# One mixture-of-experts block: first weights fetched a stage earlier, first products moved ahead of the second rows

## The reference

```python
x_mid = x + g1 * y                                   # y = merged @ w_o
h2 = modulate(rmsnorm(x_mid, norm_ffn), sh2, sc2)
g_logits = hf @ w_rg + b_rg                          # 4 groups
e_logits = hf @ w_re + b_re                          # 32 experts
...                                                  # top group, top 2 experts in it
row_tok = zeros(P).at[dest].set(tok_s)               # rows sorted by expert, blocks of 128
def run_block(tok, e, wt):
    xb = h[tok]
    y = (silu(xb @ w_g[e]) * (xb @ w_u[e])) @ w_d[e]
    return y * wt[:, None]
```

## Time and profile before

| | us |
|---|---|
| three runs, median (lowest, highest) | 1725.38 (1722.64, 1728.64) |
| the profiled execution, whole | 1726.99 |
| its span on the core | 1724.9 |
| PE busy | 1585.3 (92%) |
| DVE busy | 1181.1 (68%) |
| ACT busy | 835.0 (48%) |
| POOL busy | 185.5 (11%) |

### The profile page before, as it was taken

The page is one execution under the profiler, slowest core; times in us unless marked ns, Lnnn a source line. Parts: engine busy times, 40 slices in busy tenths (PEclk is TensorE's granted clock), DMA queues, the critical chain, the costliest instruction groups (busy, mean ns, idle before and its releaser), DMA issues. The chain is left out here.

```text
span 1724.9 us, 21049 instructions
## 1 busy us (share of the span) xinstructions
PE 1585.3 (92%) x7666; PEld 1303.0 (76%) x7666; DVE 1181.1 (68%) x1406; ACT 835.0 (48%) x912; POOL 185.5 (11%) x173
## 2 busy tenths in 40 slices
PE   7999899979939999999999999397999799999995
PEld 5789677767838888888888888276866588888883
DVE  7787866636368989898888988276666833434346
ACT  2412243362237788888888787242333523222222
POOL 0000000000021232323323231000000000000000
PEclk8999999989969999999999999698999899999998
DMA  8242344423178999999999997533102132323201
GB/s 320 89 155 87 103 147 156 166 74 101 46 285 284 367 369 366 372 378 371 378 367 368 366 369 281 198 110 120 50 27 71 52 100 93 99 96 97 98 25 49
DMA packets 121576, 329.88 MB, mean 191 GB/s; under 512 B 12601, under 2 KB 80313, under 8 KB 96817
## 3 DMA queue, kind: packets, MB, share of 16 engines
q1 hardware_dynamic: 110450, 312.11, 50.0%
q0 software_dynamic: 11072, 17.03, 2.9%
HBM read 333.00 MB, written 20.99 MB: 205 GB/s over the span
## 5 line engine op out<-in xcount | busy, mean ns | idle before, releaser
L1453 DVE TENSOR_TENSOR moe_expert_lo<-moe_expert_raw,moe_expert_hi 128x2048 fp32r<-128x2048 f32 x124 | 281.2, 2289 | 57.5 <-ACT moe_expert_hi L1275 57.5
L1275 ACT ACTIVATE moe_expert_hi<-moe_expert_raw 128x2048 fp32r<-128x2048 f32 x124 | 234.8, 1920 | 25.4 <-PE moe_bank L1548 24.0
L1535 PE MATMUL moe_bank<-moe_expert_lo,moe_x_hi 128*128 128x512 f32 x512 | 202.6, 396 | 0.0
L1536 PE MATMUL moe_bank<-moe_expert_hi,moe_x_lo 128*128 128x512 f32 x512 | 199.7, 390 | 0.0
L1537 PE MATMUL moe_bank<-moe_expert_hi,moe_x_hi 128*128 128x512 f32 x512 | 199.7, 390 | 0.0
L1865 ACT ACTIVATE second_c_hi<-second_c_raw 128x2048 fp32r<-128x2048 f32 x44 | 84.0, 1909 | 162.5 <-PE second_bank L2320 161.2
L2318 PE MATMUL second_bank<-second_cx_lo,second_c_hi 128*128 128x512 f32 x352 | 141.0, 400 | 15.4 <-DVE second_cx_lo L2015 10.2
L827 PE MATMUL mixer_bank<-mixer_h_lo,mixer_w_hi 128*128 128x512 f32 x320 | 132.2, 413 | 10.7 <-DVE mixer_h_lo L577 10.7
L2319 PE MATMUL second_bank<-second_cx_hi,second_c_lo 128*128 128x512 f32 x352 | 138.5, 393 | 0.0
L2320 PE MATMUL second_bank<-second_cx_hi,second_c_hi 128*128 128x512 f32 x352 | 138.3, 393 | 0.0
L2318 PE MATMUL second_bank<-g_lo,second_c_hi 128*128 128x512 f32 x320 | 127.4, 398 | 1.2 <-DVE g_lo L2153 1.2
(11 more groups left out here) (405 smaller groups left out, 3186.2 us busy)
## 6 DMA issues: line engine op xcount, KB each, us to landing
moe_expert_raw<-in_w_exp_up_dram SPq DMA_DIRECT2D x64, 1024.0 KB, 7.6
moe_expert_raw<-in_w_exp_down_dram SPq DMA_DIRECT2D x62, 1024.0 KB, 7.3
second_c_raw<-in_w_mlp_dram SPq DMA_DIRECT2D x32, 1024.0 KB, 5.3
moe_shared<-in_w_exp_gate_dram SPq DMA_DIRECT2D x31, 1024.0 KB, 7.1
work<-in_w_exp_gate_dram SPq DMA_DIRECT2D x31, 1024.0 KB, 7.1
mixer_raw<-in_w_in_dram SPq DMA_DIRECT2D x18, 1024.0 KB, 5.1
mixer_raw<-in_w_mod_t_dram SPq DMA_DIRECT2D x16, 1024.0 KB, 4.9
second_c_raw<-in_w_in_dram SPq DMA_DIRECT2D x8, 1024.0 KB, 8.7
```

The costliest lines, as they stand in the source:

```text
L1275: act_e.activation(w_hi[q][:], raw[r], ACT.Copy).then_inc(hi_done, 1)
L1453: dve.tensor_tensor(w_lo[q][:], raw[r], w_hi[q][:].bitcast(F32), ALU.subtract)\
L1535: pe.matmul(out, x_hi[s][:, c, :], lo[:, k, :], start=(h == 0 and k == 0), stop=False)
L1536: pe.matmul(out, x_lo[s][:, c, :], hi[:, k, :], start=False, stop=False)
```

## The change

It has four parts. `vals` and `kq` are now allocated around both stages, and four of the six raw buffers are parts of them; SP fetches the first expert's four units at the end of `mixer_stage`, behind the last `w_o` unit and a wait for the merged branches' last split (`mlo_done`). In `moe_stage` SP issues the stores first and the next expert's two gate units behind them. PE does both halves of block 0's gate ahead of `transpose_x(1, 0)`, and ACT and DVE take their splits in a matching order. In the mixer, `router(5)` and `router(6)` go into the last tile, behind chunks 3 and 6. Besides, some small tables lie in free parts of `vals` and `kq`, and DVE waits first for one of POOL's tables (`back4`), later for the rest.

```diff
@@ mixer_stage, SP
+            sp.wait_ge(mlo_done, KC)
+            for n, src in enumerate((w["w_exp_gate"], w["w_exp_gate"], w["w_exp_up"], w["w_exp_up"])):
+                sp.dma_start((vals if n < 2 else kq)[:, 2048 * (n % 2):2048 * (n % 2) + 2048],
+                             src[0].rearrange("e (p h k) f -> e h p (k f)", p=P, h=2)[0:1, n % 2])\
+                  .then_inc(expert_landed[n], 16)
@@ mixer_stage, PE
                             ins = feature_chunk(dst[:], s, k, h_hi, h_lo, c)
+                            if s == NS - 1 and k == 1 and c in (3, 6):
+                                router(KC - 3 if c == 3 else KC - 2)
...
-                    if s > 22:
+                    if s > 22 and (s, k) != (NS - 1, 1):
                         router(2 * (s - 22) + k - 2)
...
-            router(KC - 2)
@@ moe_stage
-        raw = [sb(f"expert_raw{i}", [P, 2048]) for i in range(RAW - 2)]
+        raw = [t[:, 2048 * i:2048 * i + 2048] for t in (vals, kq) for i in range(2)]
@@ moe_stage, SP
-            for n, src in enumerate((wg, wg, wu, wu)):
-                expert_unit(None, n, src, 0, n % 2)
-            expert_unit(None, 5, wg, 1, 1)
-            sp.wait_ge(xst_evac, KC)
-            expert_unit(None, 4, wg, 1, 0)
             for t in range(TC):
                 sp.wait_ge(h2_ready, t + 1)
                 sp.dma_start(dram["h2"][t * 128:(t + 1) * 128, :], h2_rows[:, t, :]).then_inc(h2_stored, 16)
+            for n in range(2):
+                expert_unit(None, 4 + n, wg, 1, n)
@@ moe_stage, POOL
-            numbers(back4[:], [[-1, 4]], 4, 0)
+            numbers(back4[:], [[-1, 4]], 4, 0).then_inc(back_ready, 1)
@@ moe_stage, ACT
             first_hi(2)
-            first_hi(3)
             act_e.wait_ge(gd_ready, 1)
             act_e.activation(gexp[:], gexp[:], ACT.Exp)
             act_e.activation(e2[:], e2[:], ACT.Exp).then_inc(gexp_ready, 1)
             x_high(0, 0)
+            first_hi(3)
+            split_hi(0, 0, 0)
             x_high(1, 1)
-            split_hi(0, 0, 0)
@@ moe_stage, DVE
-            dve.wait_ge(tables_ready, 1)
+            dve.wait_ge(back_ready, 1)
...
+            dve.wait_ge(tables_ready, 1)
             dve.tensor_tensor(chosen[:], iota_row[:, 0:32].unsqueeze(2).to_broadcast([P, 32, 8]),
...
             first_lo(1)
+            x_low(0, 0)
             first_lo(2)
-            token_gates()
-            x_low(0, 0)
-            x_low(1, 1)
             first_lo(3)
             split_lo(0, 0, 0)
+            x_low(1, 1)
+            token_gates()
             split_lo(0, 0, 1)
@@ moe_stage, PE
             pe.wait_ge(xlo_done, 1)
-            transpose_x(1, 0)
             for h in range(2):
                 pe.wait_ge(lo_done, RAW + h + 1)
                 gate_like(bank[2][:], 0, h, h).then_inc(unit_used, 1)
+            transpose_x(1, 0)
```

43 lines of the change are left out of this document (23 added, 20 removed).

## The result

| | before | after |
|---|---|---|
| runs | 12 | 12 |
| median (lowest, highest), us | 1726.59 (1722.64, 1730.61) | 1731.91 (1727.95, 1735.40) |
| ratio to before, 95% interval | | 1.0031 (1.0019 to 1.0043) |
| the profiled execution, whole / span, us | 1726.99 / 1724.9 | 1733.67 / 1731.6 |

The changed kernel is slower by some 5.3 us where 2.5 us less were forecast, and its median lies 3.4 us above the top of the range. In a second comparison the same kernel stood at 1.0023 (1.0011 to 1.0035), about 4 us.

What follows compares the result with a forecast made beforehand. The prediction took the kernel to be bound by PE, busy for 92% of the span. Its terms, 0 - 1.2 - 1.6 + 0.3, gave -2.5 us: 1722.9 us at the median, range 1718.5 to 1728.5.

Steps and rivals of the forecast that it cites:

- Item 3: First gather of rows: lands sooner because DVE pauses its weight splits; 1.2 us gained, bounds 3.0 gained to 3.1 lost.
- the gather takes the loop's time: Rival: weight units flow beside the first gather, which then takes 9.4 us as in the loop; total +1.8, 1727.2; chance 0.15.
- Item 4: First block's gate products ahead of the second block's turn: 1.6 us gained, with half clock lasting 3.7 us.
- Item 5: Two router products moved into the mixer's last tile: 0.3 us lost, bounds 0.8 lost and 0.15 gained.
- Items 1, 2, 6 and 7: First expert's early fetch, second expert's gate units behind the stores, split table wait, disturbance of x_mid's reload: no time counted.
- item 1: First expert's four units fetched in the output projection: 0 taken for the stores, other bound 0.5 us of gain.

Runs made afterwards that it cites:

- e8: Kernel before with products first and SyncE's wait for the first gather ahead of the second expert's up units, no early loads: 1725.71 us, ratio 0.9978.
- e9: Kernel before with only SyncE's wait for the first gather ahead of the second expert's up units: 1728.43 us, ratio 1.0003.
- e7: Changed kernel with routers as before, second expert's gate units ahead of the stores, its up units held until the first gather landed: 1725.67 us, ratio 0.9985.
- e13: e8 plus seven unread products inside PE's last wait of the expert loop: 1722.89 us, ratio 0.9975.
- e14: e8 plus four unread products between block 1's turn and the up products: 1725.02 us, ratio 0.9983.
- e3: Changed kernel with the second expert's gate units issued only when the first gather has landed: 1723.81 us, ratio 0.9986.
- e1: Kernel before with only the products-first orders of PE, ACT and DVE; loads, stores and routers as before: 1727.53 us, ratio 1.0006.
- e4: Changed kernel with the second expert's gate units issued ahead of the rows' stores: 1731.28 us, ratio 1.0026.
- e10: Changed kernel plus four unread products between block 1's turn and the up products: 1733.79 us, ratio 1.0036.
- e11: Changed kernel once more, unchanged, for a second profile: 1731.46 us, ratio 1.0023.
- e6: Changed kernel plus seven unread products inside PE's last wait of the expert loop: 1731.24 us, ratio 1.0018.
- e5: Changed kernel with the two router products back behind the last tile: 1730.68 us, ratio 1.0019.

## Why the prediction was wrong, point by point

**Item 3, the first gather, was the step that failed.** I took 1.2 us of gain, by a gather of 5.0 us; it cost 3.3 in the first profile and 3.1 in the second. The third gather of the earlier trace rows was the wrong one to go by, in both of its conditions. Of the kernel before, these are GpSimd's instructions for the third and the fourth gather, and the stretches from the first gather's issue to its turn and from the third's issue to its landing; the single row behind them is VectorE in the changed kernel:

```profile
514.17 1.02 POOL L1208 DMA_INDIRECT work<-h_rows_dram,moe_tok_col  x1 [0.27 <-POOL moe_tok_col L1217]
...
520.67 1.02 POOL L1208 DMA_INDIRECT work<-h_rows_dram,moe_tok_col  x1 [0.80 <-POOL moe_tok_col L1230]
...
505.27:511.70 6.43, 0.00 (x0) 0.03 (x1) 6.19 (x9) 0.07 (x1) 5.98 (x3) 0.50 0.68 228
...
514.17:519.17 5.00, 1.62 (x9) 1.65 (x9) 1.29 (x2) 0.60 (x2) 1.02 (x1) 0.50 0.65 249
```

```profile
502.90 4.49 DVE L1469 TENSOR_TENSOR moe_expert_lo<-vals,moe_expert_hi 128x2048 fp32r<-128x2048 f32 x2 [0.81 <-issue]
```

*The queues.* I read "busy, 0.74" from the average of 510 to 520 us. In the third gather's own time the share was 0.65, no more than beside the first (0.68), while in the five us behind the changed kernel's gather it was 0.97 (the last row at e8).

*VectorE.* GpSimd's instruction for the third gather took 1.02 us, for the first 1.93. That is 0.9 of the 1.3 us by which the third landed sooner. The new order could not bring it: the instruction runs in the first 1.7 to 2.7 us behind the issue, and in every run DVE splits weights all that time, in the changed kernel from 502.90 to 507.39 with the instruction from 503.82 to 506.17.

The table has the price by what flies beside the first gather: 4.2 to 5.0 us with nothing, 6.4 to 7.3 with two units, 8.6 to 9.7 with four. If the instruction's own time is taken off the landing, the three groups are tighter: 2.2 us with nothing, 4.4 to 4.7 with two, 6.1 to 7.2 with four. The fourth gather of the kernel before, in quiet queues (a share of 0.10), has the same 2.2, but it landed after 3.3 instead of 4.1 to 4.9, since its instruction took 1.02. Over all gathers of the sixteen profiles the instruction took 1.0 us in the 54 with no weight split of DVE beside it and 1.7 to 2.8 in the 474 with one. So a splitting DVE does slow the gather, as the prediction had it; what failed is that this change would relieve it. From the kernel before to the changed one (averages of two and three profiles) the instruction grew by 0.5 us and the rest of the landing by 2.5. DVE's work behind the instruction makes no difference: the rest was 2.2 where DVE split without a pause (e9) and where it paused. No run kept DVE off the first gather's instruction; by these rows that would be worth 0.6 to 1.7 us, an estimate.

The rule of the Trainium skill that I weighed against this term, "SBUF — State Buffer", "Who interferes with whom", infers that a tensor_tensor leaves descriptor writing alone. The gather's instruction was not left alone here, 1.0 against 1.7 to 2.8 us; it also reads the row numbers (`moe_tok_col`), and no run parts its reading from its writing. The other page that I weighed, "DMA: Bandwidth & Descriptors", "Queues, rings and completion order", in the Trainium skill, has each engine take turns packet by packet between the queues. That a gather should lose little to a long queue was my conclusion from it, and it did not hold: the gather lost some 2 us to each two units. No run here shows the turns themselves. The rival that I gave 0.15, "the gather takes the loop's time", priced the gather at 3.1, and that is what came.

The count of units is not the whole price. The second gathers of e7, e8, e9, e13 and e14, each with two units issued 0.6 to 1.1 us behind it, landed after 6.6 to 10.3 us, and that of e3, with four, after 7.8.

**Item 4, products first, had the right mechanism and the wrong size of clock.** The first product came 4.4 us after the turn in every kernel with this order, no weight piece was missing, and block 1's turn cost 0.8. But I let the half clock last 3.7 us from one execution. From the first product to full clock the runs had 2.9 us (e1, e4), 3.9 to 4.2 (e10, e13), 5.1 to 5.3 (e3, e7, e8, e14) and 5.8 to 6.1 (after, e11, e6, e5). T to M is then 12.15 to 13.68, against 13.97, 13.64 and 13.44 in the old order. The gain is 1.6 only with the shortest of these, and 0.4 in the changed kernel. My bounds (gain 3.4, loss 1.5) held it.

**Item 5, the routers: 0.9, not 0.3, and up to 2.5.** The piece A to S took only a few values. With the routers as before it was 37.5 or 38.3 to 38.4, with them moved 38.4, 39.2 or 40.0 to 40.1. The steps of 0.8 are a group of PE's small products at half clock or not. Here are the routers' last sums, the last router product and the stage's start in e4, both groups at half clock (1.84 and 1.90 us; 1.05 and 1.06 in e11), and then the stage's start of e7, with all of it at full clock:

```profile
475.11 1.84 PE L1009 MATMUL mixer_bank<-ones,mixer_table 128*128 128x1 f32 x8 [0.72 <-ACT mixer_table L501]
...
476.81 1.90 PE L907 MATMUL mixer_bank<-mixer_table,work 128*128 128x36 f32 x8
...
479.78 6.43 PE L1521 MATMUL moe_bank<-ident,work 128*128 128x128 f32 x32 [1.06 <-PEq L52]
```

```profile
474.85 1.06 PE L905 MATMUL mixer_bank<-mixer_table,work 128*128 128x36 f32 x8
...
476.98 6.43 PE L1521 MATMUL moe_bank<-ident,work 128*128 128x128 f32 x32 [1.06 <-PEq L52]
```

Like for like the move costs 0.9 (38.43 against 37.52), just over my bad bound; and it leaves PE two idle pieces and more late work in which the clock can fall, which I had counted as a possible gain of 0.15. Over the six kernels with it the mean is 39.36, over the ten without 37.85: 1.5 us.

**Items 1, 2, 6 and 7.** The earlier landing of the stores is worth about 0.7 (S to G 24.6 to 24.8 against 25.3 to 25.5 where the stage's turns ran alike), a little over the other bound of item 1, where I took 0. Nothing waited for units 4 and 5. The first routing step came earlier and the first token row waited 2.41 for ACT instead of 0.86: worth nothing, as said. x_mid's reload was waited for until 434.98 instead of 435.34: nothing.

**What no item had: the time behind M.** From the end of wait W to E the program is the same in all kernels, and PE took 622.5 to 627.0 us for it. The four profiles of the old order have a mean of 623.4, the twelve with the products first 626.0. That this is the doing of the order is not shown, and one row speaks against it: e8 has 626.98 in its profile, 2.8 over the mean of the two of before, and yet its ratio stands 3.8 us (1.9 to 5.5) under before, all of the 3.2 that it gained up to M. One profile's time there is not the kernel's. For a part of it the profiles show when it comes: in fourteen profiles without a filled wait the clock fell behind W in all six with a distance of 557.2 to 557.7 us from its rise, and in none of the eight with 558.0 to 559.3. The distance is fixed by the work between, counted at full clock: where the rise comes late, the products ahead of it have run at half clock, and less is left. With the products first the rise comes 2.9 to 6.1 us behind the first product, in the old order 1.9 to 2.7. With four products more the distance was 0.8 longer in e14 than in e8, and the fall went away, as its expectation says; e10 agrees. That the distance parts these profiles is shown, and in one profile each of e14 and e10 four products more took the fall away; why the chip lets the clock fall at one and not at the other is not. Nor is it shown that those with a short distance end as high as 627 for that reason: e6 filled W and ended as high, so its gain was lost again at the later waits (half clock around 1283 and 1338 there), and I could not steer those. Of the 5.3 us (4.0 in the second comparison) the pieces from A to M explain 2.4, as the next paragraph adds up; the cause of the other 1.6 to 2.9 stays open; the fall behind W, 1.6 us in both profiles of the changed kernel and absent in both of before, can be part of it.

**The sum for the changed kernel.** Piece by piece, the average of its three profiles (after, e11, and e6, which is the same program up to W) against the average of the two of before, with the forecast in brackets: A to S +0.33 (+0.3), S to G -0.78 (0), G to T +3.05 (-1.2), T to M -0.19 (-1.6); together +2.4 (-2.5). So of the error of 4.9 the gather is 4.25 and the clock in T to M 1.4, and the stores give 0.8 back. The routers' +0.33 looks like the forecast only because both profiles of before had half clock at the end of the mixer (38.3 to 38.4, not 37.5). Of the pieces that the change does not touch, end of W to E adds 626.9 against 624.2, 2.7 us, the small ones around it 0.8, and the way to A takes off 1.9 (439.9 against 441.7). Together that is the 4.0 us by which the three profiled executions are longer than the two; the medians say 5.3, the second comparison 4.0. These pieces spread by 3 to 4 us between executions of one program, so of all this only the +2.4 is pinned down, to about 1 us.

**The range** ended at 1728.5. It held the late gather, but alone, with everything else as forecast. And its bounds for the clock ended at M. Three of the misses, items 4 and 5 and the time behind M, are one: work of PE next to idle time, priced at the clock of one execution.

**The better kernel** is e8 with or without e13's filling, 0.9978 and 0.9975 of before, which are not told apart: one line that holds SyncE back until the first gather has landed, and the order of this change, without its loads and routers.

## What to carry to other kernels

Before a load is moved, look which small transfer on the critical path will then share the queues with it, and read the price from a transfer whose own few microseconds look alike, not from a stretch's average. Look at the time of the issuing instruction apart from the transfer's: VectorE's splits made it 1.7 to 2.8 us here instead of 1.0. Holding the bulk loads behind the landing of the small transfer is one line, but the transfer behind that one then pays; give PE work that doesn't need it. Where an edit moves work next to an idle stretch of PE, take a second profile of the kernel before: the clock's part differed by 3 us between two executions of the same program.
